# Turning the feed-forward strips by transposing DMAs in 16-bit halves instead of on TensorE

## What is computed

```
# block 1: D_FF = 5632
h = h + (silu(hn @ w_gate) * (hn @ w_up)) @ w_down
# block 2: D_FF_2 = 5632, a causal filter of three taps over the tokens
up = h @ w_ffn_in;  a, b = up[..., :5632], up[..., 5632:]
a = conv_w[0]*a[t-2] + conv_w[1]*a[t-1] + conv_w[2]*a[t] + conv_b
f = (gelu(a) * b) @ w_ffn_out
```

## Time and profile before

| what | value |
|---|---|
| median of three runs | 2431.97 us |
| profiled execution, first to last instruction (span) | 2429.9 us |
| TensorE busy | 2417.6 us, 99% |
| VectorE busy | 1881.4 us, 77% |
| ScalarE busy | 1387.7 us, 57% |
| granted TensorE clock, mean | 0.999 of full speed |
| DMA queue of the loads, share of 16 engines | 61.2% |

### The profile page before, as it was taken

How to read it: one execution, slowest core, us unless ns; L and a number is a source line. 1 busy time by engine, 2 the same in 40 slices (tenths; PEclk the granted TensorE clock), 3 DMA queues, 4 the chain that set the end, 5 groups by cost and what they waited for, 6 DMA issues and landing times.

```text
span 2429.9 us, 29002 instructions
## 1 busy us (share of the span) xinstructions
PE 2417.6 (99%) x11145; PEld 2008.2 (83%) x11145; DVE 1881.4 (77%) x2411; ACT 1387.7 (57%) x1744; POOL 50.6 (2%) x93
## 2 busy tenths in 40 slices
PE   9999999999999999999999999999999999999998
PEld 7888888888888888888888888888788888888887
DVE  6455555688898888989777587664889999999877
ACT  6446555445655555556456464564666666666554
POOL 1000110000000000000001100000000000000000
PEclk9999999999999999999999999999999999999999
DMA  7655555666666666666666555566566666666675
GB/s 238 198 172 155 185 156 162 217 192 191 191 197 200 201 195 203 195 192 202 197 208 198 167 154 161 155 191 197 167 197 193 196 200 188 194 195 189 200 215 169
DMA packets 239299, 460.11 MB, mean 189 GB/s; under 512 B 16582, under 2 KB 18800, under 8 KB 238528
## 3 DMA queue, kind: packets, MB, share of 16 engines
q1 hardware_dynamic: 237760, 452.65, 61.2%
q0 software_dynamic: 1376, 5.69, 0.7%
q10 hardware_dynamic: 32, 0.01, 0.0%
HBM read 456.19 MB, written 2.10 MB: 189 GB/s over the span
## 4 chain that ended last, share of the span: by engine, by line
PE 98%; DVE 1%; DMA 0%; SPq 0%; issue 0%; ACT 0%; DVEq 0%; ACTq 0%
PE acc L1005 16%; PE acc L1007 16%; PE acc L1006 16%; PE acc L721 11%; PE acc L723 11%; PE acc L722 11%; PE mis L1006 3%; PE mis L1005 3%; PE mis L1007 3%; PE mis L694 1%; PE mis L1290 1%; PE mis L819 1%; PE mis L1199 1%; PE acc L740 1%; PE acc L741 1%; PE acc L742 1%
## 5 line engine op out<-in xcount | busy, mean ns | idle before, releaser
L1601 ACT ACTIVATE wf<-wf_raw 128x1024 fp32r<-128x1024 f32 x544 | 568.4, 1058 | 548.3 <-DVE wf_raw L2431 219.1
L2443 DVE TENSOR_TENSOR wf<-wf_raw,wf 128x1024 fp32r<-128x1024 f32 x544 | 643.3, 1219 | 79.1 <-ACT wf L1601 75.6
L2099 DVE TENSOR_TENSOR lo<-raw,hi 128x1024 fp32r<-128x1024 f32 (+1 forms) x313 | 376.5, 1219 | 231.1 <-ACT hi L1354 228.7
L1354 ACT ACTIVATE hi<-raw 128x1024 fp32r<-128x1024 f32 (+1 forms) x313 | 321.0, 1049 | 162.9 <-PE acc L723 139.0
L1005 PE MATMUL acc<-wf,xb_hi 128*128 128x512 f32 x931 | 365.3, 392 | 0.0
L1007 PE MATMUL acc<-wf,xb_lo 128*128 128x512 f32 x931 | 362.7, 390 | 0.0
L1006 PE MATMUL acc<-wf,xb_hi 128*128 128x512 f32 x931 | 362.3, 389 | 0.0
L721 PE MATMUL acc<-hi,xa_hi 128*128 128x512 f32 (+1 forms) x576 | 224.4, 390 | 0.0
L723 PE MATMUL acc<-hi,xa_lo 128*128 128x512 f32 (+1 forms) x576 | 221.8, 385 | 0.0
L722 PE MATMUL acc<-lo,xa_hi 128*128 128x512 f32 (+1 forms) x576 | 221.6, 385 | 0.0
L721 PE MATMUL acc<-hi,xb_hi 128*128 128x512 f32 x544 | 216.4, 398 | 0.0
(11 more groups left out here) (530 smaller groups left out, 3800.0 us busy)
## 6 DMA issues: line engine op xcount, KB each, us to landing
raw<-in_w_in SPq DMA_DIRECT2D x215, 512.0 KB, 4.2
wf_raw<-in_w_ffn_in SPq DMA_DIRECT2D x160, 512.0 KB, 3.7
wf_raw<-in_w_gate SPq DMA_DIRECT2D x88, 512.0 KB, 3.7
wf_raw<-in_w_up SPq DMA_DIRECT2D x88, 512.0 KB, 3.8
wf_raw<-in_w_down SPq DMA_DIRECT2D x88, 512.0 KB, 4.5
wf_raw<-in_w_ffn_out SPq DMA_DIRECT2D x88, 512.0 KB, 4.0
wf_raw<-in_w_out SPq DMA_DIRECT2D x32, 512.0 KB, 4.5
raw<-in_w_o SPq DMA_DIRECT2D x32, 512.0 KB, 4.9
```

Of the source, the lines that this page charges most:

```text
L1354: nc.scalar.activation(hi[:, slot, :, 0:width], raw[:, slot, :, 0:width], ACT.Copy)\
L1601: nc.scalar.activation(wf[:, f_slot[c], 0, :, :], wf_raw[:, f_slot[c], 1, :, :], ACT.Copy)\
L2099: V.tensor_tensor(lo[:, slot, :, 0:width], raw[:, slot, :, 0:width], hi[:, slot, :, 0:width].bitcast(F32), ALU.subtract).then_inc(lo_ready, 1)
L2443: V.tensor_tensor(wf[:, f_slot[c], 1, :, :], wf_raw[:, f_slot[c], 1, :, :], wf[:, f_slot[c], 0, :, :].bitcast(F32), ALU.subtract).then_inc ...
```

## The change

A float32 value is two 16-bit halves. ScalarE now copies the halves of a staged strip into two planes of 16-bit integers (`plane_copy`, `plane_copy2`: one instruction of 128x1024 for each plane), SP issues four transposing DMAs for each strip (two planes by two token tiles, 128x512 of 16 bits each), and ScalarE writes the turned planes back into the halves of float32 words (`ff_copy`, `joined`: again one instruction of 128x1024 for each plane). The TensorE transposes are gone for all strips but the last two of block 2, which are still turned in `e0` at k = 2.

```
# SP, inside the loop over k and behind it
+ if p.stage == "ffn" and p.i and k == 7:  turn_planes(p.i - 1)
+ if p is d0 and k == 8:                   turn_planes(FT - 1)
+ if p.stage == "ffn2" and k == 7:         turn_planes2(p.i - 1, 0)
  for h in range(2): ... load chunk (k, h)
...
+ if p.stage == "ffn2":                    turn_planes2(p.i - 1, 1)   # behind (7,1)
+ def turn_planes2(m, j):
+     sp.wait_ge(planes2_ok[j], 2 * m + 2)
+     for h in range(2):
+         for t in range(TT):
+             sp.dma_start(tplanes2[j][:, h, :, t*P:(t+1)*P], planes2[j][:, h, t, :], transpose=True)\
+                 .then_inc(planes2_turned[j], 16)
# TensorE
- if p in ffn_b and k == p.nk - 1:
-     pe.wait_ge(y_ok, p.no + 1)
-     turn(i2 + p.i - 1, stg, 1)
- if p is d0 and k == 2: ... turn(i3 - 1, stg, 1)
- if p.wide and k == p.nk - 1: ... turn_half(p.i - 1, 0); between = turn_b
# ScalarE, block 1, pair i
  t_hi_of(p, 3)
+ plane_copy(p.i - 1, 0)
  f_hi_of(p, 4, 1)
  f_hi_of(p, 5, 0)
+ plane_copy(p.i - 1, 1)
  f_hi_of(p, 5, 1)
...
  ff_copy(p.i - 1)            # now two copies of 128x1024 from the turned planes
# ScalarE, block 2, pair i
  t_hi_of(p, 3)
+ plane_copy2(p.i - 1, 0, 0)
  f_hi_of(p, 4, 1)
+ plane_copy2(p.i - 1, 0, 1)
  gelu(p.i - 2)
  f_hi_of(p, 5, 0)
+ plane_copy2(p.i - 1, 1, 0)
  f_hi_of(p, 5, 1)
+ plane_copy2(p.i - 1, 1, 1)
  f_hi_of(p, 6, 0)
  t_hi_of(p, 5)
...
  f_hi_of(after, 0, 0)
  f_hi_of(after, 0, 1)
- turned_copy(p.i - 1, 0)
+ joined(p.i - 1, 0)          # waits for planes2_turned[0], two copies of 128x1024
  t_hi_of(after, 0)
- turned_copy(p.i - 1, 1)
+ joined(p.i - 1, 1)          # waits for planes2_turned[1]
  f_hi_of(after, 1, 0)
# VectorE
  def gated_up(p): ...
+     dve.wait_ge(planes_ok, 2 * p.i)
```

More of the change, by code:

```diff
@@ L29 @@
 I32 = mybir.dt.int32
+U16 = mybir.dt.uint16
 ALU = mybir.AluOpType
@@ L234, in two_blocks @@
         ff_raw = at("ff_raw", A0, [KF, T])
+        planes2 = [at(f"planes2_{j}", A0 + (KF - 8 + 4 * j) * T, [2, TT, W], U16) for j in range(2)]
         ff_lo = at("ff_in_place_lo", A0, [KF, T], F32R)
@@ L379, in two_blocks @@
         p1_out, v_ok, x_ok, u_ok, y_ok = sem("p1_out"), sem("v_ok"), sem("x_ok"), sem("u_ok"), sem("y_ok")
+        planes_ok, planes_turned = sem("planes_ok"), sem("planes_turned")
+        planes2_ok = [sem(f"planes2_ok{j}") for j in range(2)]
+        planes2_turned = [sem(f"planes2_turned{j}") for j in range(2)]
         tile_sum, gate_ok, ff_out = sem("tile_sum"), sem("gate_ok"), sem("ff_out")
@@ L566, in stages, with turns, halves_of @@
             return 2 * (item + 1)
+        def turns(item):
+            i2, i3 = PH["ffn"][2], PH["down"][2]
+            return item + 1 - (FT if item >= i3 else 0)
+        def halves_of(words):
+            pairs_of = words.bitcast(U16).rearrange("p a (w h) -> p a w h", h=2)
+            return [pairs_of[:, :, :, h] for h in range(2)]
         def needs(c, t):
@@ L639, in _, with turn_planes @@
             couple("branch", w_a, w_b, 0, 0, 8, DT)
+            def turn_planes(m):
+                sp.wait_ge(planes_ok, 2 * m + 2)
+                if m:
+                    sp.wait_ge(ff_out, m)
+                for h in range(2):
+                    for t in range(TT):
+                        sp.dma_start(tplanes[:, h, :, t * P:(t + 1) * P], planes[:, h, t, :], transpose=True)\
+                            .then_inc(planes_turned, 16)
+            def turn_planes2(m, j):
+                sp.wait_ge(planes2_ok[j], 2 * m + 2)
+                for h in range(2):
+                    for t in range(TT):
+                        sp.dma_start(tplanes2[j][:, h, :, t * P:(t + 1) * P], planes2[j][:, h, t, :], transpose=True)\
+                            .then_inc(planes2_turned[j], 16)
             def pair_chunks(p):
                 for k in range(p.nk):
+                    if p.stage == "ffn" and p.i and k == 7:
+                        turn_planes(p.i - 1)
+                    if p is d0 and k == 8:
+                        turn_planes(FT - 1)
+                    if p.stage == "ffn2" and k == 7:
+                        turn_planes2(p.i - 1, 0)
                     for h in range(2):
@@ L1024, in touch @@
                         pe.wait_ge(tile_sum, 4 * p.no)
-                turned_out = FT if not p.wide else max(p.i - F_FIRST, 0) if p.stage != "out" else 0
+                turned_out = FT if p.run and not p.wide else 0
                 if name == "p1" and p in (out0, f1):
@@ L1305, in _ @@
                 for k in range(p.nk):
[L1306 to L1310, removed]
                     if p is e0 and k == 2:
-                        pe.wait_ge(a_in, FT - 1)
+                        pe.wait_ge(p1_out, e0.no)
+                        pe.wait_ge(x_ok, e0.no)
                         turn_half(FT - 1, 0)
-                        pe.wait_ge(b_in, FT - 1)
+                        pe.wait_ge(y_ok, e0.no)
                         turn_half(FT - 1, 1)
@@ L1616, in gates_on, with plane_copy @@
                 last.then_inc(gate_ok, 1)
+            def plane_copy(m, h):
+                act.wait_ge(staged, stages(i2 + m))
+                if m and h == 0:
+                    act.wait_ge(planes_turned, 64 * m)
+                nc.scalar.activation(planes[:, h, :, :], halves_of(stg[:, :, :])[h], ACT.Copy).then_inc(planes_ok, 1)
             def ff_copy(m):
[L1620 to L1623, removed]
+                act.wait_ge(planes_turned, 64 * (m + 1))
+                for h in range(2):
+                    last = nc.scalar.activation(halves_of(ff_raw[:, 4 * m:4 * m + 4, :])[h], tplanes[:, h, :, :],
+                                                ACT.Copy)
                 last.then_inc(ff_out, 1)
@@ L1764, in _ @@
                         gates_on(ffn_b[-1])
-                    if p is d0 and k == 5:
+                    if p is d0 and k in (3, 5):
+                        plane_copy(FT - 1, k // 4)
+                    if p is d0 and k == 11:
                         ff_copy(FT - 1)
@@ L1971, in scaled, with plane_copy2, joined @@
                     last.then_inc(staged, 1)
+            def plane_copy2(m, j, h):
+                act.wait_ge(staged, stages(PH["ffn2"][2] + m) - 1 + j)
+                nc.scalar.activation(planes2[j][:, h, :, :], halves_of((stg, stg2)[j][:, :, :])[h], ACT.Copy)\
+                    .then_inc(planes2_ok[j], 1)
+            def joined(m, j):
+                act.wait_ge(planes2_turned[j], 64 * (m + 1))
+                act.wait_ge(ff_out, FT + m)
+                for h in range(2):
+                    last = nc.scalar.activation(halves_of((a_sb, b_sb)[j][:, :, :])[h], tplanes2[j][:, h, :, :], ACT.Copy)
+                last.then_inc((a_in, b_in)[j], 1)
             def turned_copy(m, pair):
-                act.wait_ge((a_turned, b_turned)[pair], m + 1)
+                act.wait_ge((a_turned, b_turned)[pair], 1)
                 act.wait_ge(ff_out, FT + m)
```

26 lines of the change are left out of this document (14 added, 12 removed).

## The result

The changed kernel took 2477.43 us (median of 4 runs, 2475.89 to 2479.53) against 2431.97: a ratio of 1.0187 [1.0175, 1.0200], 45 us slower, where 2425 had been forecast and 2456 was the upper end of the range. The profiled execution took 2476.04 us.

A forecast was written before the change was run, and what follows sets the result against it. TensorE bounds the kernel (99% busy); in block 2 VectorE and ScalarE would become the bound. Block 1's -9.6 us and block 2's +2.5 sum to -7.1 on 2431.97, about 2425 us; range 2404 to 2456.

The forecast's parts named there:

- TensorE's part: Both blocks: 31 transpose groups of 0.87 us removed, 27.0 us, leaving TensorE 41.5 and 41.6 us a pair.
- Start of the next pair: Block 2, ScalarE's list from split through both joins to the split of (1,0): VectorE's L2443 starts 0.32 us later.
- step 5: Block 2: the fourth plane copy delays L1608 by 0.98 us and VectorE's L2450 by 0.8; TensorE has 0.66 in hand.
- has none of this: Block 1: the extra copies and new waits cost nothing, all 11 groups are saved, -9.6 us.
- ScalarE's copies: A 16-bit copy of 128x1024 taken at 0.98 us, like float; +2.9 us a block-1 pair, +5.9 in block 2.
- the wait of the filter: Block 2, VectorE's wait for L1985: shrinks from 1.41 us to about 0.1 if TensorE gets ahead.
- SP's issue: SP's queue: 0.37 us per issue, as for a load; wait before L2430 0 to 1.5 us, 0.5 taken.
- second rival: Issues hold back the loads: from about t = 1.0 us each no gain; 2452 us at t = 1.5; chance 0.28.
- VectorE's idle time: Block 2: 2.9 us a pair before the change, which makes VectorE and ScalarE the bound at 43.05 us.
- DMA engines: Four transposes move 512 KB a strip: 1.7 us of all 16 engines taken, 12.8 if every 256-byte piece is a packet.
- third rival: Transposes fill the DMA engines: 53 us of DMA work a block-2 pair, +10 each, +100 us; chance 0.12.
- first rival: Everything is saved, TensorE stays the bound: -27.0 us, 2405 us; chance 0.18 for everything or most saved.

The follow-up runs named there:

- e3: Changed kernel without its 124 transposing DMAs; plane copies and joins kept, so strips are not turned: 2429.2 us.
- e13: Changed kernel with VectorE's half of chunk (1,0) put behind finish and finish_up in both blocks, scaled waiting for the joins: 2438.97 us.
- e15: Changed kernel with the e13 order, two transposing DMAs a strip, and block 2's joins and second-strip DMAs moved as in e8: 2408.8 us, ratio 0.9903.
- e14: Kernel before the change with only VectorE's half of chunk (1,0) put behind finish and finish_up: 2431.90 us, ratio 0.9998.
- e5: Changed kernel with each join made as two dense 128x512 copies of 32-bit words, writing zeros: 2446.46 us.
- e7: Changed kernel with block 2's joins moved behind the split of (1,0) and the next pair's first filter tap, last plane copy moved later in step 5: 2450.66 us.
- e8: e7 with block 2's second-strip transposing DMAs also moved behind the loads of the next pair's step 0: 2424.23 us.
- e4: Changed kernel with its 124 transposing DMAs replaced by plain DMAs of the same bytes between the same places: 2456.24 us.
- e16: e5 and e13 together on the changed kernel, short joins and finish ahead of (1,0): 2426.33 us.
- e6: Changed kernel with block 2 back on TensorE, block 1's DMAs moved behind the next pair's step 0 loads and ff_copy to a later step 2: 2429.22 us, ratio 0.9988.
- e9: Changed kernel with the moves of e6 in block 1 and of e8 in block 2: 2421.1 us, ratio 0.9956.
- e11: e10 with one transposing DMA of 128x1024 per token tile, two a strip instead of four: 2410.67 us, ratio 0.9914.
- e10: e9 with VectorE's half of chunk (1,0) put behind finish and finish_up in both blocks: 2414.81 us, ratio 0.9927.
- e12: Changed kernel with two transposing DMAs of 128x1024 a strip instead of four of 128x512, placed as in the change: 2468.33 us.

## Why the prediction was wrong

Block 2 was forecast at 43.55 us a pair and took 47.54; block 1 at 41.5 and took 42.47. In the order of its steps:

- **TensorE's part** held: 41.4 us a pair where nothing else is late (e3, e13, e15 in block 1), and e15 shows that most of it can be had in block 2.
- **The step that failed: "Start of the next pair".** It followed ScalarE's list to the split of (1,0) and VectorE's list to the half that waits for it, and stopped there with "+0.32 us", booked on VectorE's list only. It didn't ask who waits for what stands behind: `finish`, and behind it TensorE. By its own numbers `finish` comes 0.3 later and TensorE 0.9 earlier, and the trace of before has 0.79 in hand: a wait of 0.4 already. The same check was made for step 5 only ("TensorE has 0.66 us in hand here"), where no wait is seen in the pair above. TensorE late means buffers free late, loads late, VectorE late, and `finish` later still: the chain of waits goes round that way in the pair above, from 1997.62 over the load of (7,1) at 2022.71 to the sums at 2034.45. That the circle sets the period in every pair is my reading; that `finish` behind (1,0) is a part of it is shown by e13 and e14. Out of the circle, in e13, block 2 takes 44.68: 2.9 of the 4.0 us that the forecast was short by are this step's, what the low clock costs among them.
- **Block 1, "has none of this"**: the same kind of omission, at another instruction. Its joins do stand behind `t_hi` and cost nothing (e5), but beside the DMAs the load of (7,1) lands late (4.8 us after its issue instead of 3.6, medians), and `t_lo_of`, for which TensorE waits, stands behind the half of (1,0) there. Without the DMAs block 1 is at 41.39 (e3), with them and (1,0) last at 41.34 (e13).
- **ScalarE's copies.** Plane copies take 1.04 us (1.06 was the row taken). The two copies of a join take 1.35 each and hold the list for 2.43 (1987.89 to 1990.32), where 1.95 was taken. Two joins stand in the chain, +0.9 us. The other effects came as worked out: (1,0) waits 1.58 us (1.47 predicted), `t_lo` of step 5 waits 0.73 (0.8), and the wait of the filter is gone. VectorE's list of that pair (start, us, instruction, [idle before]):

```profile
1991.81 1.76 DVE L2511 TENSOR_TENSOR tf<-tf_raw,tf 128x1536 fp32r<-128x1536 f32 x1 [0.66 <-ACT tf L1640]
1995.14 1.23 DVE L2504 TENSOR_TENSOR wf<-wf_raw,wf 128x1024 fp32r<-128x1024 f32 x1 [1.58 <-ACT wf L1633]
...
2000.95 1.67 DVE L3043 SCALAR_TENSOR_TENSOR ff_raw<-a_sb,vec,ff_raw 128x255 f32<-128x255 f32 x4
...
2021.79 1.76 DVE L2511 TENSOR_TENSOR tf<-tf_raw,tf 128x1536 fp32r<-128x1536 f32 x1 [0.73 <-ACT tf L1640]
```

- **SP's issue** was taken at the 0.37 us of a plain load and is 1.27. The wait for the load of step 0 is 17.3 us in 7.8 pairs, 2.2, where 0.5 was taken: the second rival's mechanism, which it had decide from t = 1.0. The rival's price was misadded: 2040.1 + 4 x 1.5 + 0.4 is 2046.5 and not 2046.9, so t = 1.5 is a wait of 2.5 and not 2.9. By the same terms t = 1.27 gives 1.6. With that for 0.5 the sum of the forecast is 44.65, and e13 has 44.68; that it comes so close is in part luck, since the single waits differ. Moving four DMAs away gave 2.2 (e7 to e8). That their issues do it and not their packets is seen in the landing of (0,1), unchanged at 4.6 us. The Trainium skill (DMA: Bandwidth & Descriptors, the table of the accelerated DGE) had led to an estimate of 1.2 us; the trace agrees, with 1.27.
- **VectorE's idle time** is 6.9 us a pair where the steps summed to 2.9: 2.9 before L2504 (22.4 / 7.8; 1.5 forecast), 2.2 before L2491 (0.5), 1.4 before L2511 (0.8). What L2504 has more than (1,0)'s wait is a second one a pair, behind the late load of (7,1).
- **DMA engines.** The share of the loads' queue gives (63.4% x 2474.3 - 61.2% x 2429.9) / 31 = 2.6 us of 16 engines per strip, by 67456 / 124 = 544 packets a DMA, where 1.7 was taken and 12.8 was the far end. The third rival is refuted: the share is 0.73 in the pair shown, and e15 runs at 0.85 without harm. The Trainium skill (Advanced Engine Details and Errata, X-Bar Transpose) calls such DMAs as fast as regular ones, and the runs agree: the plain DMAs of e4 with the same bytes cost 2.4 us a strip by the same sum and land after 4.3 us (median; 4.2 with the transpose). Both cost more than the 1.7 that was taken from the loads' longer rows.
- **The clock.** That TensorE's idle time can be followed by microseconds at the lower level was in no term: 1.8 us in the pair shown, at most 0.9 a pair on the mean. Low stretches are all but gone from block 2 in e3, e5, e7 and e13 (one or none in 1800 to 2170), so each of their gains of about 3 us holds up to 0.9 of it. They don't add up either way: e5 and e13 together give 4.1 (e16) and not 6.0, since both take away the wait for `finish`; the moves of the joins and of the second strip's DMAs give 5.05 together (e8).
- **The first rival** (everything saved) gave 2405; e15 comes to 2408.8, by an order that the change doesn't have.

Still open: which part of what stays in e6 and e9 to e11 (block 1 at 42.0, and 41.6 in e11, with its DMAs moved; 41.4 in e13 and e15, with them in the change's place) is due to the DMAs' new place and which to `ff_copy`'s; they were only moved together.

## What to carry to other kernels

When work moves from the bounding engine to its helpers, follow each helper's list past the instruction that comes late to everything queued behind it, and check for each whom it releases and with how much in hand; here a margin of 0.79 us before a product that had never waited, used up unseen, was the larger part of the miss. A DMA has a price on the queue that issues it, and it is paid by the loads behind it: putting four of them behind the loads that were due next gave 2.2 us a pair in block 2. It is no rule without exception: block 1 did better with its DMAs in the change's place (41.34 in e13) than moved (42.08 in e10). And look for the free reordering first: the half of (1,0) moved in VectorE's lists was worth 38 us with the change (one execution) and nothing without it.

## What the runs showed of the hardware

- A transposing DMA of 128x512 16-bit elements from SBUF to SBUF holds its issuing queue for 1.27 us (1.19 at least), one of 128x1024 for 1.85 to 2.17 (medians of e12 and e11, block 2; 1.24 at least), a plain DMA of as many bytes as the first 0.64 to 0.68 (e4), a plain load 0.37. The one of 128x512 lands after 2.5 to 7.0 us and is moved as 544 packets.
- On ScalarE, a copy of 128x1024 16-bit integers read with a stride of two takes 1.04 us, written with a stride of two 1.35; float32 contiguous takes 1.06 (the changed kernel's trace).
- In one pair TensorE's granted clock fell to half within 1 us behind an idle stretch of 1.45 us, and stayed there for about 7 us, through another of 1.63. It was low for a while in six of nine such pairs and stayed full in the other three; no idle stretch of TensorE in them was longer than 2.35 us.
